# A hybrid encoder layer on one core: the opening written in another order on TensorE, VectorE and ScalarE

## What is computed

```python
mod = jax.nn.silu(c) @ w_ada[l] + b_ada[l]
sh1, sc1, g1, sh2, sc2, g2, sh3, sc3, g3 = jnp.split(mod, N_MOD, axis=-1)

h = modulate(rms_norm(x, ffn1_norm[l]), sh1, sc1)     # h * (1 + scale) + shift
x = x + 0.5 * g1[:, None, :] * swiglu(h, ffn1_w1[l], ffn1_w3[l], ffn1_w2[l])
...
y = jnp.concatenate([o_hg, o_rg], axis=-1) @ w_out[l]
x = x + g2[:, None, :] * y
...
return rms_norm(x, final_norm)
```

## Time and profile before

| | us |
|---|---|
| median of 3 runs | 1025.04 |
| lowest and highest | 1024.93, 1028.9 |
| the profiled execution | 1029.99 |
| its span | 1028.3 |
| TensorE busy | 998.1 (97%) |
| VectorE busy | 750.3 (73%) |
| ScalarE busy | 505.0 (49%) |
| first triple of the opening starts | 26.05 |
| gate product of units 0 and 1 starts | 50.50 |

### The profile page before, as it was taken

How to read it: one execution, slowest core, us unless ns; L and a number is a source line. 1 busy time by engine, 2 the same in 40 slices (tenths; PEclk the granted TensorE clock), 3 DMA queues, 4 the chain that set the end, 5 groups by cost and what they waited for, 6 DMA issues and landing times.

```text
span 1028.3 us, 18555 instructions
## 1 busy us (share of the span) xinstructions
PE 998.1 (97%) x6946; PEld 868.3 (84%) x6946; DVE 750.3 (73%) x1039; ACT 505.0 (49%) x691; POOL 229.0 (22%) x191
## 2 busy tenths in 40 slices
PE   7999999999999999999999989999999999999997
PEld 5779999999888787777677667878999999988887
DVE  6777878877788768678899994567778787783334
ACT  5555444444323234687878953465434344433221
POOL 0024454452123210101000000202435354200100
PEclk9999999999999999999999999999999999999999
DMA  9557667765787826421121301235576767653322
GB/s 355 203 177 200 164 196 201 182 188 167 256 290 269 321 86 241 143 83 62 47 79 45 96 27 63 82 115 154 151 175 184 188 175 206 197 173 100 103 82 83
DMA packets 63190, 162.21 MB, mean 158 GB/s; under 512 B 5440, under 2 KB 7760, under 8 KB 63008
## 3 DMA queue, kind: packets, MB, share of 16 engines
q1 hardware_dynamic: 44720, 110.79, 30.5%
q0 software_dynamic: 18416, 50.68, 20.6%
HBM read 159.36 MB, written 2.10 MB: 157 GB/s over the span
## 4 chain that ended last, share of the span: by engine, by line
PE 77%; issue 8%; DVE 7%; ACT 3%; DMA 3%; POOL 1%; SPq 1%; DVEq 0%; POOLq 0%; ACTq 0%
PE psum L1884 13%; PE psum L1886 13%; PE psum L1885 13%; PE psum L1956 10%; PE psum L1958 10%; PE psum L1957 10%; DMA raw<-wu 1%; DMA sraw_a<-ws 1%; DMA raw<-ws 1%; DVE dif L1643 1%; PE psum L2185 1%; DVE wlo L1353 1%; PE psum L2187 1%; PE psum L2186 1%; PE psum L2214 1%
## 5 line engine op out<-in xcount | busy, mean ns | idle before, releaser
L580 ACT ACTIVATE whi<-raw 128x1024 fp32r<-128x1024 f32 x92 | 97.3, 1057 | 227.2 <-PE psum L1886 209.1
L1102 DVE TENSOR_TENSOR wlo<-raw,whi 128x1024 fp32r<-128x1024 f32 x94 | 118.5, 1260 | 120.2 <-ACT whi L580 119.7
L1886 PE MATMUL psum<-ghi,wlo 128*128 128x512 f32 (+2 forms) x384 | 143.7, 374 | 0.0
L1885 PE MATMUL psum<-glo,whi 128*128 128x512 f32 (+2 forms) x384 | 143.4, 373 | 0.0
L1884 PE MATMUL psum<-ghi,whi 128*128 128x512 f32 (+2 forms) x384 | 143.0, 372 | 0.0
L1884 PE MATMUL psum<-hhi,whi 128*128 128x512 f32 x320 | 130.7, 408 | 3.0 <-DVE wlo L1102 1.3
L1886 PE MATMUL psum<-hhi,wlo 128*128 128x512 f32 x320 | 125.0, 391 | 0.0
L1885 PE MATMUL psum<-hlo,whi 128*128 128x512 f32 x320 | 124.9, 390 | 0.0
L1956 PE MATMUL psum<-forms,whi 128*128 128x256 f32 x432 | 121.1, 280 | 0.0
L1957 PE MATMUL psum<-forms,whi 128*128 128x256 f32 x432 | 120.5, 279 | 0.0
L1958 PE MATMUL psum<-forms,wlo 128*128 128x256 f32 x432 | 120.5, 279 | 0.0
(11 more groups left out here) (266 smaller groups left out, 2347.1 us busy)
## 6 DMA issues: line engine op xcount, KB each, us to landing
raw<-wu SPq DMA_DIRECT2D x96, 512.0 KB, 3.4
ada<-wada POOLq DMA_DIRECT2D x56, 512.0 KB, 5.3
sraw_a<-ws SPq DMA_DIRECT2D x36, 512.0 KB, 6.2
raw<-ws SPq DMA_DIRECT2D x36, 512.0 KB, 6.5
sraw_b<-ws SPq DMA_DIRECT2D x36, 256.0 KB, 4.3
sraw_a<-ws POOLq DMA_DIRECT2D x18, 512.0 KB, 6.0
raw<-ws POOLq DMA_DIRECT2D x18, 512.0 KB, 6.0
early<-wada SPq DMA_DIRECT2D x16, 512.0 KB, 15.2
```

What stands on the lines that cost most here:

```text
L580: nc.scalar.activation(whi[:, slot, :], raw[:, slot, :], ACT.Copy).then_inc(hi_done, 1)
L1102: nc.vector.tensor_tensor(wlo[:, slot, :], raw[:, slot, :], whi[:, slot, :], ALU.subtract).then_inc(lo_done, 1)
L1885: nc.tensor.matmul(dst, a, rlo, start=False, stop=False)
L1886: return nc.tensor.matmul(dst, b, rhi, start=False, stop=stop)
```

## The change

On **ScalarE** the root comes before the copy of block 0's rows; the load of the Silu table comes before the weight copies; the row copies of blocks 1 and 2 and the copy of unit 3's weights come later.

On **VectorE** the reciprocal comes before the small vectors; ten of the small steps (now in `bound_values`) go behind the last tile of the opening; the row sum of block 0 comes before the two weight splits, which now stand around the first `hlo`; the split of units 2 and 3 moves in the same way, and the row sum of block 2 behind them.

On **TensorE** the two halves of a block's products are pulled apart, with triples between them; the order of the triples is another; and fillers are moved and added: 2 + 3 + 4 behind the norm sums before, 3 + 10 + 4 + 6 now.

```diff
             act.wait_ge(ones_set, 2)
+            root(0)
             rows_copy(0)
-            root(0)
+            nc.scalar.preload_act_table(ACT.Silu)
             hi(0, 0)
             hi(0, 1)
-            nc.scalar.preload_act_table(ACT.Silu)
-            rows_copy(1)
             first_h(0)
             first_h(1)
             h_copy(0, 0)
             h_copy(0, 1)
+            rows_copy(1)
             hi_extra(0)
-            hi_extra(1)
             first_h(2)
             first_h(3)
-            rows_copy(2)
+            hi_extra(1)
             h_copy(0, 2)
             h_copy(0, 3)
+            rows_copy(2)
...
                 step(nc.vector.tensor_scalar(half_gain, vec("hg_norm"), 0.5, None, ALU.mult))
+
+            def bound_values():
+
                 step(nc.vector.tensor_tensor(t8, lb_e[:, 0:8], lb_e[:, 8:16], ALU.add))
...
             add_first_squares(1)
+            rms_inverse(0, rms_done, rinv_done)
             small_values()
-            rms_inverse(0, rms_done, rinv_done)
-            lo(0, 0)
-            lo(0, 1)
             rows_add(0)
             for q in range(BLOCKS):
                 block_columns(q)
...
                 first_tmp(2 * q)
                 first_tmp(2 * q + 1)
+                if q == 0:
+                    lo(0, 0)
                 first_lower(2 * q)
                 if q == 0:
+                    lo(0, 1)
+                if q == 1:
+                    lower_extra(0)
+                first_lower(2 * q + 1)
+                if q == 0:
                     rows_add(1)
-                first_lower(2 * q + 1)
                 if q == 1:
+                    lower_extra(1)
                     rows_add(2)
-                if q in (0, 1):
-                    lower_extra(q)
                 if q == 2:
                     late_rows()
+            bound_values()
             ffn_up(0)
...
             first_norm_sums(1)
             block_rows(0, 0)
-            keep_busy(7, 2)
             norm_rb(0)
             block_rows(0, 1)
             keep_busy(3, 3)
             block_sums(0)
+            keep_busy(3, 10)
             block_rows(1, 0)
-            block_rows(1, 1)
             keep_busy(3, 4)
             first_unit(0, range(0, 1))
+            block_rows(1, 1)
+            first_unit(1, range(0, 1))
+            first_unit(0, range(1, 2))
             block_sums(1)
-            first_unit(0, range(1, 2))
-            first_unit(1, range(0, 2))
+            first_unit(1, range(1, 2))
+            keep_busy(3, 6)
             block_rows(2, 0)
+            for k in (2, 3):
+                first_unit(0, range(k, k + 1))
+                first_unit(1, range(k, k + 1))
+                first_unit(2, range(k - 2, k - 1))
             block_rows(2, 1)
-            first_unit(2, range(0, 2))
+            first_unit(3, range(0, 2))
             block_sums(2)
-            first_unit(0, range(2, 4))
-            first_unit(1, range(2, 4))
-            first_unit(3, range(0, 2))
             first_unit(2, range(2, 4))
             first_unit(3, range(2, 4))
             for u in range(4):
```

## The result

| | before | changed |
|---|---|---|
| median of 7 runs, us | 1025.93 | 1031.92 |
| lowest and highest | 1024.93, 1028.9 | 1030.37, 1036.18 |
| ratio to before, 95% interval | | 1.0064 [1.0044, 1.0083] |
| the profiled execution, and its span | 1029.99, 1028.3 | 1031.91, 1030.2 |
| second norm sums start | 13.20 | 13.84 |

A forecast was written before the change was run, and what follows sets the result against it. TensorE, busy 97% of the span, was taken as the bound. The new wait for tile 6 makes the opening 1.55 us longer, small steps and clock add nothing: +1.5, so 1026.5 us, range 1023.9 to 1029.0.

The forecast's parts named there:

- The clock: Granted clock in the opening: full clock expected, worth nothing; a half-rate stretch behind the new wait would cost 1.7 us.
- the last block: From block 2's sums to tile 6: 11.76 us chain, TensorE waits about 2.5 us, begins tile 6 1.55 us later.
- I see nothing that makes it more than 1.7 at full clock: Upper bound claimed for the opening's shift at full clock, itself forecast at 1.55 us, or 1.15 with free turns.
- The shift is the same for both: The +1.5 us applies alike to profiled execution (1029.99 to 1031.5) and median (1025.04 to 1026.5).
- Root and spread: Start of the opening: the earlier root lets the spread follow at 15.2 us, not 16.39, so 1.2 us sooner.
- row sum: Block 0 on VectorE: no longer behind two weight splits, so block 0's sums start at 18.1, 2.55 us sooner.
- first triple: First three-matmul group on TensorE in the opening: starts at 23.3 us and not 26.05.
- Third block: Block 2's sums on TensorE start at 37.3 us where they started at 34.15, 3.15 us later.
- Tile 6: End of the opening: TensorE waits about 2.5 us for it and begins it at 49.1, not 47.55.
- Full clock: Opening's shift without a clock fall: 1.55 us later, and not more than 1.7.
- rival 2: Wait brings the clock down, or ten fillers between 19 and 21 us don't hold it: +3.2 us, 1028.2, chance 0.22.
- Small steps: Ten VectorE steps, 1.9 us, moved behind the last tile: hidden before the gate product, with 0.35 us to spare.

The follow-up runs named there:

- e6_old_pe_late_sums: Changed kernel with TensorE's old order and fillers, but block 2's second half of products and its sums still late among the triples; 1030.06 us, ratio 1.0051.
- e10_after_few_fillers: Changed kernel without the ten fillers ahead of block 1's products and the six ahead of block 2's; 1032.1 us, ratio 1.0057.
- e14_after_3: The changed kernel run a third time with no edit; 1032.09 us, ratio 1.0074.
- e2_sums_early: Changed kernel with the second half of block 2's products and its sums placed earlier on TensorE; 1027.8 us, ratio 1.0019.
- e3_late_split: Changed kernel with two of the last block's four row products on VectorE moved in front of block 2's row sum; 1028.37 us, ratio 1.0026.
- e15_old_pe_2: Same kernel as e5_old_pe (changed kernel with TensorE's order and fillers of before), run again in another job; 1028.29 us, ratio 1.0025.
- e5_old_pe: Changed kernel with TensorE's order and fillers of before, VectorE and ScalarE as changed; 1025.94 us, ratio 0.9996.
- e7_few_fillers: e2_sums_early without the ten fillers ahead of block 1's products and the six ahead of block 2's; 1025.16 us, ratio 1.0001.
- e9_few_split: e7_few_fillers with one of the four late row products on VectorE moved sooner, behind block 2's row sum; 1025.6 us, ratio 0.9994.
- e12_late_sums_2: Same kernel as e6_old_pe_late_sums, run again in another job; 1030.93 us, ratio 1.0061.

## Why the prediction was wrong

The step that failed is **"The clock"**: it put the fall behind the wait for tile 6 at nothing in the sum, and the opening of the changed kernel pays some 1.6 us for each fall. With it failed the sentence under the last block, "I see nothing that makes it more than 1.7 at full clock": that term measured 2.4. Those two bring the forecast of +1.5 to about +4.1; the rest of the measured +6.0 lies in the step "The shift is the same for both", and its cause is open. The mechanism of the wait itself was right.

- *Root and spread, row sum, first triple.* Right. Less the 0.64 us of later norm sums: spread 15.17 (forecast 15.2), sums of block 0 18.20 (18.1), first triple 23.43 (23.3).
- *Third block.* Right in kind and nearly in size: 37.67 for 37.3.
- *Tile 6.* Right: a wait of 2.24 us (about 2.5). But it ends at 36.73 us behind the norm sums, where 35.86 was forecast. 0.37 us of that are the sums; 0.50 are in the chain from sums to tile 6, 12.26 us long and not 11.76: 0.35 for the pause of VectorE at 40.05, and 0.15 from the end of `hlo` to the matmul, which the 11.76 left out. I took a chain from the old order as fixed. The wait is 2.24 and not 2.5 because TensorE comes to tile 6 later too; it had waited 0.39 us for tile 4, which the forecast had at nothing.
- *Full clock.* With these, the opening is 2.4 us longer (`e14_after_3`) and not 1.55: the term was short by 0.9, and the bound of 1.7 false.
- *Clock.* I weighed the fall as rival 2 with 0.22 and the dense matmuls on both sides against it. It comes in two of three traces of the changed kernel, in both of the kernel of `e6_old_pe_late_sums` and in `e10_after_few_fillers`, and the ordinary runs of the kernels that wait show 1.1 stretches more than those of the kernel before. So the case that I gave 0.22 was the usual one. The Trainium skill ("TensorE: Matmul & The Clock Gate", "Part 1: The HAM clock gate") says throttled is the default and activity releases it; that leaves room for the fall, and five of the six traces that have the wait show it, `e14_after_3` doesn't. An early fall between 14.1 and 15.0 us, which the forecast did not have, comes in 7 of the 17 traces, in neither of the kernel before, and costs the new order about 1.6 us (42.89 against 41.25). The fall of the kernel before, at 21.5 and 22.3 us, had the DMA wait until 31.66 behind it to be absorbed in, and the new order has used that wait up.
- *Small steps.* Right: hidden, 2.2 us to spare.
- *"The shift is the same for both".* Not held. The opening's distance grew on average by 4.1 us over the three traces (39.74, 41.25, 42.89 against 37.18), which is the forecast 1.55, 0.9 of chain and sums, and some 1.6 of clock. The medians grew by 6.0, 7.2 and 6.7 us. I let one profiled execution stand for the median, though a half-rate stretch near 612 and waits for late weights move an execution by 1.6 to 4.8 us.

**What is still open:** 2 to 3 of the 6 to 7 us. The dear place of the stretch near 612 in both profiles of the kernel before could be up to 1.6 of them; that is argued, not shown. The new order of VectorE and ScalarE could be part of them as well: of the kernels that have it and don't wait for tile 6, `e2_sums_early`, `e3_late_split` and `e15_old_pe_2` are 2.0 to 2.9 us over before, though `e5_old_pe`, `e7_few_fillers` and `e9_few_split` are within 0.7 us of it. No run has the change in TensorE alone. Whether a later opening makes late-landing weights more frequent can't be told from one profile of each kernel, and two jobs of one kernel differ by 2.4 us.

## What to carry over

When a reordering brings starts forward, follow the one product whose consumer chain is longest (here 12 us from the sums of block 2 to tile 6) and count what remains behind it for the busy engine, not what was won in front. Price a new wait between dense matmuls with a fall of the clock behind it, as the likely case where the traces show falls behind shorter ones, and remember that slack which can hide an old fall may be gone. Lay two traces over each other matmul by matmul before an end is put down to a change: many of the profiles here had 1.6 to 4.8 us of their own. Where a kernel's own runs spread over 5 us and the effect is 2, run the pair in one job.

## What the chip showed that I had not expected

- A 2.2 us wait with dense 128x512 matmuls on both sides goes with 3.4 us of TensorE at 1.2 GHz in five of the six traces that have the wait, and not in `e14_after_3`; they begin between 0.2 us ahead of the wait's end and 1.1 us behind it. With eight fillers inside the wait none of three traces has the fall.
- The same kernel falls to half rate at 14.1 to 15.0 us in some runs and not in others, though TensorE has short matmuls there throughout (`e12_late_sums_2`: busy 3.40 of 3.40 us).
- One of a 512 KB load's 16 parts landed 3.1 us behind the other fifteen, and the load behind it did the same (fifteen by 67.64, the last at 71.68). DMA was busy all along (columns as above):

```profile
60.19:66.45 6.26, 6.26 (x29) 5.15 (x28) 5.43 (x6) 2.12 (x2) 1.37 (x1) 1.00 0.98 351
66.45:69.54 3.09, 3.09 (x15) 2.55 (x14) 0.00 (x0) 0.00 (x0) 0.00 (x0) 1.00 1.04 186
```

- VectorE paused 0.40 us between two dependent steps (39.65 to 40.05) in all 13 traces with one list of its instructions, at the same place of the list, and 0.04 in the four with another (`e3_late_split`, 40.14 to 40.17); what makes it was not tried.
